# Attention of an encoder layer on one core: probabilities transposed in 64-row tiles, scores issued one at a time over three banks, chunks kept in a ring of twelve slots

## The chip, the core and the metric

The kernel runs on one core of a Trainium2 chip. The metric is the device time of one execution in microseconds (us), the median of three runs. TensorE (PE) does matmuls and transposes into PSUM, which has eight banks of 128 x 512 float32. VectorE (DVE), ScalarE (ACT) and GpSimd (POOL) work on PSUM and SBUF, SyncE issues DMAs. Each engine works through its own queue in order, and the queues are tied together by semaphores that the kernel waits on by hand.

## The reference, cut to what matters

One encoder layer over 1024 tokens of width 1024 in float32. Only the two attentions are touched by the change:

```
h = rmsnorm(x, norm1_g);  proj = h @ w_in         # queries, keys, values, pooling input
o_a = neighbourhood_attention(...)                # 4 heads of 64, 16 columns x 8 rows around each token
o_b = sliding_window_gqa(...)                     # 8 query heads on 2 key heads, |distance| <= 128, ALiBi, sink
o_c = multiscale_pool(...)
x = x + concat(o_a, o_b, o_c) @ w_out
x = x + hierarchical_moe(rmsnorm(x, norm2_g), ...)   # 32 experts, two for each token
out = rmsnorm(x, final_g)
```

For each head the attentions are softmax(q k + bias) v.

## The kernel before

The work runs in stages: projections, attention, output projection, routing, the 32 experts, the sum. Attention is a software pipeline over 96 **units**. A unit is one head of one **step**; a step is a block of 128 queries with four heads and 256 (at the edges) or 384 keys. There are 8 steps of neighbourhood attention ("na", one per block) and then 16 of sliding window attention ("swa", two groups of four heads per block). `attention_plan()` lays the work out over ticks; at tick u each engine runs its part of the list:

- PE: when u is a multiple of 4, the scores of the four units of a step (`scores`, L809 and L814): keys and queries have 64 features, heads with even number lie on partitions 0 to 63, odd ones on 64 to 127, and each unit has one of the banks 0 to 3. Unit u waits until unit u - 4 has left its bank (`bias_done`). In ticks 0, 2, 4 and 6 it still does parts of the last projection (`last_high`, L781).
- DVE: `bias_and_max(u)` (L1514, L1526) reads the scores from PSUM, adds the bias table and writes them to SBUF; the reciprocal of the sum of unit u - 2, and for some units its normalising multiply (L1550).
- ACT: the exponentials of unit u (L1177).
- POOL: the normalising multiply of the other units (L2039), three in four of swa.

Eleven to fourteen ticks after tick 4s of its scores a step comes to its transposes and its products. For each **chunk** of 128 keys PE transposes the four 128 x 128 blocks of probabilities (`transposes`, L829) into one bank (one of 4, 5, 7 in turn), DVE or ACT copies the bank to SBUF (`evacuate_chunk`, L485 and L490), and PE multiplies with the values (`times_values`, L847 for na, L853 for swa, where one product serves both groups) into bank 6; ACT copies the result out (L1190). There are 22 chunks of na and 44 of swa. The copies go to two sets of buffers, `ptna` and `ptswa`, and wait until the step two before has been multiplied (`pv_done`). In the list, the transposes of a step come first, then the products of the step before. DVE makes 25 of the 66 copies, ACT 41.

On DVE's queue the order within a tick is bias, reciprocal, multiply, and last the copy of the chunk that PE transposes in the same tick; the next tick's bias stands behind it. Two ticks after the last unit PE does the four pooling products (`pooled`, L859) into banks 0 to 3.

Of the kernel before, what the change touches and what calls it, by code (L numbers as in the profile page):

```python
# [26 lines left out]
F32 = mybir.dt.float32  # L27
# [5 lines left out]
P = 128  # L33
# [55 lines left out]
def attention_plan():  # L89


    steps = []
    for i in range(TT):
        lo, hi = max(i - 1, 0), min(i + 2, TT)
        steps.append(("na", i, 0, lo * P, (hi - lo) * P))
    for b in range(TT):
        lo, hi = max(b - 1, 0), min(b + 2, TT)
        for g in range(SWA_KV):
            steps.append(("swa", b, g, lo * P, (hi - lo) * P))
    lag = 8  # L100
    ticks = [[] for _ in range(4 * len(steps) + lag + 4)]
    late = []
    for s, (kind, i, g, k0, nk) in enumerate(steps):
        nc_ = -(-nk // P)
        items = []
        for c0 in range(0, nc_, GROUP):
            group = range(c0, min(c0 + GROUP, nc_))
            items += [("T", s, c) for c in group]
            items += late
            late = [("V", s, c) for c in group] if kind == "na" or g == 1 else []  # L110
        if s == len(steps) - 1:
            items += late
        for j, it in enumerate(items):
            ticks[4 * s + 3 + lag + (4 * j) // len(items)].append(it)
    return steps, ticks


def encoder(nc, x, norm1_g, w_in, nat_tab, swa_sink, pool_w, pool_scale, w_out, norm2_g,
# [8 lines left out]
    with ExitStack() as ctx:  # L127
# [8 lines left out]
        def sem(name):  # L136
# [62 lines left out]
        pswa = [at(f"pswa{i}", [P, 4, 3 * P + 1], F32, off) for i, off in enumerate((H + 56 * KB, TD + 8 * KB, TMP, Q + 8 * KB))]  # L199
        ptna = [at(f"ptna{i}", [P, 5, 512], F32, W + 4 * KB + i * 10 * KB) for i in range(2)]  # L200
        ptswa = [[at(f"ptswa{i}_{c}", [P, 2, 512], F32, W + 4 * KB * (1 + 3 * i + c) if 3 * i + c < 5 else Q) for c in range(3)]
                 for i in range(2)]

# [193 lines left out]

        def by_vector(n):

            return n % 2 == 0 if n < na_chunks else n % 3 == 0  # L400

        def tbank(n):

            return (4, 5, 7)[n % 3]

        VBANK = 6

        def chunk_ready(eng, n):

            if n >= 0:  # L410
                mine = by_vector(n)
                eng.wait_ge(pt_v if mine else pt_a, sum(by_vector(m) == mine for m in range(n + 1)))

# [22 lines left out]
        def sbank(u):  # L436
            return u % 4

# [36 lines left out]

        def evacuate_chunk(eng, copy, done, s, c):

            n = chunk_no[(s, c)]
            kind, i, g, k0, nk = steps[s]
            w = min(P, nk - c * P)  # L480
            eng.wait_ge(tr_done, n + 1)
            if kind == "na":
                if s >= 2:
                    eng.wait_ge(pv_done, vnum[(s - 2, last_chunk[s - 2])] + 1)
                copy(ptna[s % 2][0:w, c, :], ps[0:w, tbank(n), :]).then_inc(done, 1)  # L485
            else:

                before = NA_STEPS - 2 + i if i < 2 else NA_STEPS + 2 * (i - 2) + 1
                eng.wait_ge(pv_done, vnum[(before, last_chunk[before])] + 1)
                copy(ptswa[i % 2][c][:, g, :], ps[:, tbank(n), :]).then_inc(done, 1)  # L490

# [197 lines left out]
        def _(pe):  # L689
# [111 lines left out]
            def scores(u):  # L801
                s, h = u // 4, u % 4
                kind, i, g, k0, nk = steps[s]
                if s < NA_STEPS:
                    if u >= 4:
                        pe.wait_ge(bias_done, u - 3)
                    q = qa[(h % 2) * HD:(h % 2 + 1) * HD, h // 2, i * P:(i + 1) * P]
                    k = ka[(h % 2) * HD:(h % 2 + 1) * HD, h // 2, k0:k0 + nk]
                    mm = nc.tensor.matmul(ps[:, sbank(u), 0:nk], q, k, start=True, stop=True)  # L809
                else:  # L810
                    pe.wait_ge(bias_done, u - 3)
                    hh = 4 * g + h
                    rows = slice((hh % 2) * HD, (hh % 2 + 1) * HD)
                    mm = nc.tensor.matmul(ps[:, sbank(u), 0:nk], qs[rows, hh // 2, i * P:(i + 1) * P], kb[rows, g, k0:k0 + nk],  # L814
                                          start=True, stop=True)
                mm.then_inc(score_done, 1)

            def transposes(s, c):
                n = chunk_no[(s, c)]
                w = min(P, steps[s][4] - c * P)  # L820
                if c == 0:
                    pe.wait_ge(norm_p, sum(not norm_by_vector(u) for u in range(4 * s + 4)))
                    pe.wait_ge(norm_v, sum(norm_by_vector(u) for u in range(4 * s + 4)))
                if n == 2:
                    pe.wait_ge(proj_out, 2 * MT)
                else:
                    chunk_ready(pe, max((m for m in range(n) if tbank(m) == tbank(n)), default=-1))
                for h in range(4):
                    mm = nc.tensor.transpose(ps[0:w, tbank(n), h * P:(h + 1) * P],  # L829
                                             pbuf(4 * s + h)[:, c * P:c * P + w], ident[:])  # L830
                mm.then_inc(tr_done, 1)

            def times_values(s, c):
                kind, i, g, k0, nk = steps[s]
                oi = o_steps.index(s)
                w = min(P, nk - c * P)
                tile = k0 // P + c
                chunk_ready(pe, chunk_no[(s, c)])
                if c == 0 and oi == 0:
# [4 lines left out]
                if kind == "na":  # L844
                    for h in range(4):
                        half = slice((h % 2) * HD, (h % 2 + 1) * HD)
                        mm = nc.tensor.matmul(bank[half, (h // 2) * P:(h // 2 + 1) * P],  # L847
                                              vtok[0:w, tile, h * HD:(h + 1) * HD], ptna[s % 2][0:w, c, h * P:(h + 1) * P],
                                              start=(c == 0 and h < 2), stop=(c == last_chunk[s]), skip_group_check=True)
                else:  # L850
                    chunk_ready(pe, chunk_no[(s - 1, c)])
                    for gg in range(2):
                        mm = nc.tensor.matmul(bank[gg * HD:(gg + 1) * HD, :], vtok[:, tile, 256 + gg * HD:256 + (gg + 1) * HD],  # L853
                                              ptswa[i % 2][c][:, gg, :], start=(c == 0), stop=(c == last_chunk[s]))
                mm.then_inc(pv_done, 1)

            def pooled(i, n):
                pe.wait_ge(pool_step, POOL_OPS)
                mm = nc.tensor.matmul(ps[:, 2 * i + n, :], pwd[:, i, :], cu[:, i, PAD + n * 512:PAD + (n + 1) * 512],  # L859
                                      start=True, stop=True)  # L860
# [3 lines left out]
            pe.wait_ge(proj_out, PROJ.index((ORDER.index(3), 1)) + 1)  # L864
            pe.wait_ge(const_in, 16 * 9)
            for u, tick in enumerate(ticks):
                if u < NU and u % 4 == 0:
                    for h in range(4):
                        scores(u + h)
                if u in (0, 2, 4, 6):  # L870
# [3 lines left out]
                if u == NU + POOL_LAG:  # L874
                    pe.wait_ge(bias_done, NU)
                    for i in range(2):
                        for n in range(2):
                            pooled(i, n)
                for kind, s, c in tick:
# [235 lines left out]
        def _(act):  # L1115
# [76 lines left out]
            def wo_high(n, k):  # L1192
                c = n * KT + k
                act.wait_ge(wo_in[wo_count(c)], 32 * max(c // 4, 1))
                nc.scalar.copy(wohi[n][:, k, :], woraw[wo_buf(c)][:]).then_inc(wohi_done[n], 1)

            pending = []
            for u, tick in enumerate(ticks):
                if u < NU:
                    exponentials(u)  # L1200
                if u == NU + POOL_LAG:
                    act.wait_ge(const_in, 16 * 9)
                    for i in range(2):
                        for n in range(2):
                            act.wait_ge(pool_mm, 2 * i + n + 1)
                            nc.scalar.mul(oT[:, 6 + i, n * 512:(n + 1) * 512], ps[:, 2 * i + n, :],
                                          pscale[:, i:i + 1]).then_inc(pool_out, 1)
                for s in pending:
                    o_evacuate(s)
                pending = []  # L1210
                for kind, s, c in tick:
                    if kind == "T" and not by_vector(chunk_no[(s, c)]):
                        evacuate_chunk(act, nc.scalar.copy, pt_a, s, c)
                    if kind == "T" and chunk_no[(s, c)] == len(chunk_no) - 1:
# [164 lines left out]
        def _(dve):  # L1379
# [163 lines left out]
            for u, tick in enumerate(ticks):  # L1543
# [642 lines left out]
```

## Time and profile before

| | |
|---|---|
| median of 3 runs | 731.18 us (730.85 to 731.6) |
| the profiled execution: time, span of its instructions | 730.85 us, 729.0 us |
| mean granted TensorE clock | 0.992 |
| attention, from its first scores to its last product | 166.64 to 283.05 us of the span |
| PE busy over the span | 97% |

A granted clock of 1 means 2.4 GHz; it is 1.00 in all of attention. In the profile's rows a busy time of PE counts the matmuls' latency too, so PE can read 100% busy while it waits a little; the chain of work that ended last gives each piece only the time until the next one starts, and the pieces add up. A float32 matmul shows as two records there, a transpose as one.

### The profile page before, as it was taken

How to read it: one execution, taken by the hardware profiler on the slowest of the kernel's cores; microseconds unless marked ns; L12 is line 12 of the kernel's file. 1: busy time of each engine (PE TensorE's matmuls, PEld its weight loads, DVE VectorE, ACT ScalarE, POOL GpSimd, SP SyncE). 2: the span in 40 equal slices, each digit the busy share in tenths (PEclk: the TensorE clock that was granted, in tenths of full speed). 3: DMA queues.
4: the chain of work that ended last, by engine and by line, in shares of the span. 5: the costliest groups of instructions: out<-in, count | busy, mean ns of one | idle time of the engine just before them, and what ended most of it. 6: DMA issues, size and time to landing. Idle time of an engine off the chain costs nothing.

```text
span 729.0 us, 10252 instructions
## 1 busy us (share of the span) xinstructions
PE 704.2 (97%) x3757; PEld 511.3 (70%) x3757; DVE 508.0 (70%) x811; ACT 390.1 (54%) x585; POOL 321.8 (44%) x241
## 2 busy tenths in 40 slices
PE   7999999999999999999999899999999999999983
PEld 6888888886775556888889666666666666666631
DVE  5646422215988887214377898888888888888977
ACT  6500000104888887001122688888888888887815
POOL 2423458953778771610000454444444444442213
PEclk9999999999999999999999999999999999999997
DMA  9422112100400003705666599999999999999978
GB/s 308 140 58 58 32 55 59 30 0 23 123 1 1 1 1 140 206 5 200 230 227 207 178 351 385 390 384 381 383 383 384 390 383 383 385 386 379 400 273 350
DMA packets 62419, 157.74 MB, mean 216 GB/s; under 512 B 10168, under 2 KB 24992, under 8 KB 62368
## 3 DMA queue, kind: packets, MB, share of 16 engines
q1 hardware_dynamic: 55728, 139.58, 52.9%
q0 software_dynamic: 6336, 16.89, 7.0%
q8 instruction: 31, 0.51, 0.3%
q10 hardware_dynamic: 304, 0.59, 0.2%
q14 instruction: 20, 0.16, 0.1%
HBM read 142.36 MB, written 18.87 MB: 221 GB/s over the span
## 4 chain that ended last, share of the span: by engine, by line
PE 88%; DMA 5%; DVE 3%; SPq 1%; issue 1%; ACT 1%; POOL 0%; DVEq 0%; POOLq 0%
PE ps L1008 7%; PE ps L1013 7%; PE ps L1016 7%; PE ps L727 6%; PE ps L725 6%; PE ps L726 6%; PE ps L829 4%; PE ps L891 4%; PE ps L893 4%; PE ps L892 4%; PE ps L1039 4%; PE ps L1043 4%; PE ps L1035 4%; PE ps L814 3%; DMA wd<-in_expert_w_down 3%; PE ps L853 3%
## 5 line engine op out<-in xcount | busy, mean ns | idle before, releaser
L1810 DVE TENSOR_TENSOR wgulo<-wgu,unit 128x2048 fp32r<-128x2048 f32 x64 | 146.2, 2286 | 26.4 <-ACT unit L1276 26.4
L1276 ACT CAST unit<-wgu 128x2048 fp32r<-128x2048 f32 x64 | 122.2, 1910 | 3.7 <-PE ps L949 1.6
L2084 POOL DMA_INDIRECT expert_rows<-ysb,idx x32 | 70.8, 2212 | 108.2 <-ACT ysb L1323 107.2
L2077 POOL DMA_INDIRECT xg<-h_rows,idx x32 | 59.2, 1849 | 71.2 <-PE ps L984 58.3
L725 PE MATMUL ps<-hThi,whi 128*128 128x512 f32 x200 | 78.3, 392 | 0.0
L727 PE MATMUL ps<-hThi,wlo 128*128 128x512 f32 x200 | 77.9, 389 | 0.0
L726 PE MATMUL ps<-hTlo,whi 128*128 128x512 f32 x200 | 77.8, 389 | 0.0
L1816 DVE TENSOR_TENSOR wdlo<-wd,unit 128x2048 fp32r<-128x2048 f32 x32 | 73.1, 2285 | 2.6 <-ACT unit L1285 2.5
L1008 PE MATMUL ps<-unit,xThi 128*80 128x512 f32 x256 | 70.9, 398 | 0.8 <-ACT xThi L1300 0.8
L1013 PE MATMUL ps<-unit,xTlo 128*80 128x512 f32 x256 | 69.2, 391 | 0.0
L1016 PE MATMUL ps<-wgulo,xThi 128*80 128x512 f32 x256 | 69.1, 391 | 0.0
L1285 ACT CAST unit<-wd 128x2048 fp32r<-128x2048 f32 x32 | 61.1, 1909 | 4.8 <-DMA wd<-in_expert_w_down 4.8
L2039 POOL TENSOR_SCALAR pswa<-pswa,esum 128x384 f32<-128x384 f32 (+1 forms) x48 | 55.9, 1182 | 12.8 <-DVE esum L1533 12.8
L1137 ACT COPY kb<-ps 64x512 f32<-64x512 f32 x8 | 4.7, 583 | 92.6 <-DVE ps L1410 92.5
L1013 PEld LDWEIGHTS ps<-unit,xTlo 128*80 128x80 f32 x256 | 37.8, 148 | 21.1 <-DVE xTlo L1823 0.2
L1016 PEld LDWEIGHTS ps<-wgulo,xThi 128*80 128x80 f32 x256 | 37.8, 148 | 21.1
L891 PE MATMUL ps<-wohi,oThi 128*128 128x512 f32 x128 | 51.3, 401 | 0.0
L893 PE MATMUL ps<-wohi,oTlo 128*128 128x512 f32 x128 | 50.0, 391 | 0.0
L892 PE MATMUL ps<-wolo,oThi 128*128 128x512 f32 x128 | 49.9, 390 | 0.0
L1008 PEld LDWEIGHTS ps<-unit,xThi 128*80 128x80 f32 x256 | 35.4, 149 | 16.7 <-ACT xThi L1300 0.9
L1177 ACT ACTIVATE pswa<-pswa,mneg 128x385 f32<-128x385 f32 (+1 forms) x64 | 37.6, 588 | 13.0 <-DVE mneg L1526 12.8
L1972 POOL TENSOR_SCALAR stat<-stat 128x1 f32<-128x1 f32 x16 | 5.5, 344 | 87.8 <-ACT h L1249 65.3
(226 smaller groups left out, 1449.4 us busy)
## 6 DMA issues: line engine op xcount, KB each, us to landing
wgu<-in_expert_w_gate SPq DMA_DIRECT2D x64, 512.0 KB, 12.4
wgu<-in_expert_w_up SPq DMA_DIRECT2D x64, 512.0 KB, 15.3
wd<-in_expert_w_down SPq DMA_DIRECT2D x32, 1024.0 KB, 17.5
y<-expert_rows SPq DMA_DIRECT2D x16, 512.0 KB, 9.8
wraw<-in_w_in SPq DMA_DIRECT2D x14, 512.0 KB, 3.9
xin<-in_x SPq DMA_DIRECT2D x8, 512.0 KB, 6.7
x<-in_x SPq DMA_DIRECT2D x8, 512.0 KB, 7.3
out<-fo SPq DMA_DIRECT2D x8, 512.0 KB, 3.3
```

What stands on the lines that cost most here:

```text
L725: nc.tensor.matmul(bank, whi[i % 2][:, k, :], hThi[:, k, cols], start=(k == 0), stop=False)
L726: nc.tensor.matmul(bank, whi[i % 2][:, k, :], hTlo[:, k, cols], start=False, stop=False)
L727: mm = nc.tensor.matmul(bank, wlo[i % 2][:, k, :], hThi[:, k, cols], start=False, stop=(k == KT - 1))
L891: nc.tensor.matmul(ps[:, g % 4, :], oThi[t][:, k, :], wohi[n][:, k, :], start=(k == 0), stop=False)
L892: nc.tensor.matmul(ps[:, g % 4, :], oThi[t][:, k, :], wolo[n][:, k, :], start=False, stop=False)
L893: mm = nc.tensor.matmul(ps[:, g % 4, :], oTlo[t][:, k, :], wohi[n][:, k, :], start=False, stop=(k == KT - 1))
L1008: nc.tensor.matmul(bank, xThi[e % 2][:, 4 * a + k, :], hi[:, :, k * DE:(k + 1) * DE], start=(a == 0 and k == 0), stop=False)
L1013: nc.tensor.matmul(bank, xTlo[e % 2][:, 4 * a + k, :], hi[:, :, k * DE:(k + 1) * DE], start=False, stop=False)
L1016: mm = nc.tensor.matmul(bank, xThi[e % 2][:, 4 * a + k, :], lo[:, :, k * DE:(k + 1) * DE], start=False, stop=(a == 1 and k == 3))
L1276: nc.scalar.copy(weight_unit(e, a)[:], raw_half(wgu, e, a)).then_inc(ahi_done, 1)
L1810: nc.vector.tensor_tensor(raw_half(wgulo, e, a), raw_half(wgu, e, a), weight_unit(e, a)[:].bitcast(F32), ALU.subtract).then_inc(alo_done, 1)
L1816: nc.vector.tensor_tensor(wdlo[e % RING][:].rearrange("p j d -> p (j d)").rearrange("p (a f) -> p a f", a=2), wd[e % RING][:].rearrange("p ...
```

## The change

Four edits, all in attention:

1. Each 128 x 128 transpose becomes two, of 64 query rows each (partitions 0 to 63 and 64 to 127), written to the two banks of a pair, (3, 4) or (5, 7). Two chunks in a row share a pair: bank one then holds queries 0 to 63 of both chunks and four heads, bank two queries 64 to 127. A copy moves one such bank, after both chunks have been transposed. DVE makes 25 of these 66 copies (never the second bank of a pair), ACT 41. PE may use a pair of banks again when both copies of the pair two before are done, and the products of a chunk wait for both copies of its pair.
2. The copies go to one ring of twelve slots `pt`, one for each chunk; a slot is reused when its reader twelve chunks before is done.
3. Scores are issued one unit per tick, two ticks ahead of DVE (unit u + 2 at the head of tick u), over banks 0 to 2; a unit waits until the unit three before it has left its bank.
4. The plan puts one chunk's transposes into each of the first three ticks of a step and all products of the step before into the fourth. The fourth pooling product uses bank 0 again and comes a tick later.

```diff
-GROUP = 3
+SLOTS = 12
+AHEAD = 2
...
-        for j, it in enumerate(items):
-            ticks[4 * s + 3 + lag + (4 * j) // len(items)].append(it)
+        first = 4 * s + 3 + lag
+        for c in range(nc_):
+            ticks[first + c].append(("T", s, c))
+        ticks[first + 3] += late
+        late = [("V", s, c) for c in range(nc_)] if kind == "na" or g == 1 else []
...
-            return n % 2 == 0 if n < na_chunks else n % 3 == 0
+        def by_vector(pair, half):
+            return half == 0 and (2 * pair < na_chunks or pair % 3 != 2)
...
+        def tbanks(pair):
+            return ((3, 4), (5, 7))[pair % 2]
...
         def sbank(u):
-            return u % 4
+            return u % 3
...
+        def evacuate_pair(eng, copy, done, pair, half):
+            n = 2 * pair
+            eng.wait_ge(tr_done, n + 2)
+            if n >= SLOTS:
+                eng.wait_ge(pv_done, max(reader(n - SLOTS), reader(n + 1 - SLOTS)))
+            j = n % SLOTS
+            copy(pt[:, j:j + 2, :].rearrange("p c (h x q) -> p c h x q", h=4, x=2)[:, :, :, half],
+                 ps[:, tbanks(pair)[half], :].rearrange("p (c h q) -> p c h q", c=2, h=4)).then_inc(done, 1)
...
-                    pe.wait_ge(bias_done, u - 3)
+                    pe.wait_ge(bias_done, u - 2)
...
                 for h in range(4):
-                    mm = nc.tensor.transpose(ps[0:w, tbank(n), h * P:(h + 1) * P],
-                                             pbuf(4 * s + h)[:, c * P:c * P + w], ident[:])
+                    for half in range(2):
+                        rows = slice(half * HD, (half + 1) * HD)
+                        o = (n % 2) * 256 + h * HD
+                        mm = nc.tensor.transpose(ps[:, tbanks(pair)[half], o:o + HD],
+                                                 pbuf(4 * s + h)[rows, c * P:(c + 1) * P], ident[rows, rows])
...
+            first_units = {0: (0, 1, 2), 1: (), 2: (3, 4), 3: (), 4: (5, 6), 5: (), 6: (7, 8), 7: (9,)}
             for u, tick in enumerate(ticks):
-                if u < NU and u % 4 == 0:
-                    for h in range(4):
-                        scores(u + h)
+                for x in first_units.get(u, (u + AHEAD,)):
+                    if x < NU:
+                        scores(x)
...
-                    if kind == "T" and by_vector(chunk_no[(s, c)]):
-                        evacuate_chunk(dve, nc.vector.tensor_copy, pt_v, s, c)
+                    if kind == "T" and chunk_no[(s, c)] % 2 == 1 and by_vector(chunk_no[(s, c)] // 2, 0):
+                        evacuate_pair(dve, nc.vector.tensor_copy, pt_v, chunk_no[(s, c)] // 2, 0)
```

## Rows read from the trace of the kernel before

**Rows 1.** The page: busy time of each engine, and the granted clock in 40 slices.
```profile
PE 704.2 (97%) x3757; PEld 511.3 (70%) x3757; DVE 508.0 (70%) x811; ACT 390.1 (54%) x585; POOL 321.8 (44%) x241
...
PEclk9999999999999999999999999999999999999997
```

**Rows 2.** The chain that ended last, whole attention: start, length (us), piece.
```profile
166.71 1.06 PE ps L809 x8
...
186.39 1.02 PE ps L847 x16
...
215.58 1.02 PE ps L847 x16
...
260.07 2.73 PE ps L853 x12
```

**Rows 3.** The same chain, one block of swa (eight units).
```profile
235.08 1.49 PE ps L814 x8
236.57 2.06 PE ps L829 x16
238.63 1.98 PE ps L814 x8
240.61 0.59 PE ps L829 x4
241.20 2.72 PE ps L853 x12
243.92 0.59 PE ps L829 x4
244.51 0.52 PE ps L814
```

**Rows 4.** Busy time of each engine in that block.
```profile
235.08:244.51 9.43, 9.43 (x54) 4.98 (x54) 7.63 (x30) 7.52 (x22) 7.45 (x7) 1.00 0.01 2
```

**Rows 5.** The chain, one step of na (four units).
```profile
188.44 1.49 PE ps L809 x8
189.93 0.59 PE ps L829 x4
190.52 1.46 PE ps L847 x24
191.98 1.02 PE ps L829 x8
193.00 0.52 PE ps L809
```

**Rows 6.** The chain, end of attention.
```profile
272.81 3.44 PE ps L859 x8
...
280.47 0.59 ACT ptswa L490
```

**Rows 7.** The chain, one expert: transposes of 80 rows into 80 columns.
```profile
425.80 0.56 PE ps L984 x8
```

**Rows 8.** Timeline in the block of rows 3: start, length, engine, operation.
```profile
237.23 0.68 DVE L490 COPY ptswa<-ps 128x512 f32<-128x512 f32 x1
...
237.83 0.61 DVE L1526 CUSTOM_DVE_ANT_0 pswa<-ps,dist,nsink 128x384 f32<-128x384 f32 x1
...
238.56 0.30 PEld L814 LDWEIGHTS ps<-kb,qs 64*128 64x128 f32 x4 [0.17 <-DVE mneg L1526]
...
239.70 0.29 PEld L814 LDWEIGHTS ps<-kb,qs 64*128 64x128 f32 x2 [0.20 <-DVE mneg L1526]
...
240.54 0.42 PEld L829 LDWEIGHTS ps<-ident,pswa 128*128 128x128 f32 x4 [0.55 <-issue]
```

**Rows 9.** Timeline in na: a chunk's four transposes and DVE's copy of it.
```profile
185.74 0.66 PE L829 MATMUL ps<-ident,pna 128*128 128x128 f32 x4
...
186.43 0.69 DVE L485 COPY ptna<-ps 128x512 f32<-128x512 f32 x1
```

**Rows 10.** Groups of the attention stage by line and shape: busy us, mean ns of one.
```profile
L1526 DVE CUSTOM_DVE_ANT_0 pswa<-ps,dist,nsink 128x384 f32<-128x384 f32 x48 | 29.0, 604 | 0.4
...
L1514 DVE CUSTOM_DVE_ANT_0 pna<-ps,ti 128x384 f32<-128x384 f32 x20 | 10.9, 543 | 2.6 <-PE ps L809 2.6
```

More of the change, by code:

```diff
@@ L104, in attention_plan @@
         nc_ = -(-nk // P)
[L105 to L110, printed above, removed]
+        first = 4 * s + 3 + lag
[3 more added lines that the diff above has]
+        late = [("V", s, c) for c in range(nc_)] if kind == "na" or g == 1 else []
         if s == len(steps) - 1:
-            items += late
-        for j, it in enumerate(items):
-            ticks[4 * s + 3 + lag + (4 * j) // len(items)].append(it)
+            ticks[first + nc_ - 1] += late
     return steps, ticks
@@ L199, in encoder @@
         pswa = [at(f"pswa{i}", [P, 4, 3 * P + 1], F32, off) for i, off in enumerate((H + 56 * KB, TD + 8 * KB, TMP, Q + 8 * KB))]
[L200 to L202 removed]
+        pt = at("pt", [P, SLOTS, 512], F32, W)
         pa = at("pa", [P, S + 2 * PAD], F32, TMP)
@@ L396, in encoder, with pair_ready, reader @@
         na_chunks = sum(s < NA_STEPS for s, _ in chunk_no)
-        def by_vector(n):
-            return n % 2 == 0 if n < na_chunks else n % 3 == 0
-        def tbank(n):
-            return (4, 5, 7)[n % 3]
+        def by_vector(pair, half):
+            return half == 0 and (2 * pair < na_chunks or pair % 3 != 2)
+        def tbanks(pair):
+            return ((3, 4), (5, 7))[pair % 2]
         VBANK = 6
[L408 to L412, printed above, removed]
+        def pair_ready(eng, pair):
+            if pair >= 0:
+                n_v = sum(by_vector(m, half) for m in range(pair + 1) for half in range(2))
+                eng.wait_ge(pt_v, n_v)
+                eng.wait_ge(pt_a, 2 * (pair + 1) - n_v)
+        def reader(n):
+            s, c = next(k for k in chunk_no if chunk_no[k] == n)
+            if steps[s][0] == "swa" and steps[s][2] == 0:
+                s += 1
+            return vnum[(s, c)] + 1
         def norm_by_vector(u):
@@ L819, in transposes @@
                 n = chunk_no[(s, c)]
-                w = min(P, steps[s][4] - c * P)
+                pair = n // 2
                 if c == 0:
@@ L875, in _ @@
                     pe.wait_ge(bias_done, NU)
-                    for i in range(2):
-                        for n in range(2):
-                            pooled(i, n)
+                    pooled(0, 0)
+                    pooled(0, 1)
+                    pooled(1, 0)
+                if u == NU + POOL_LAG + 1:
+                    pooled(1, 1)
                 for kind, s, c in tick:
@@ L1202, in _ @@
                     act.wait_ge(const_in, 16 * 9)
[L1203 to L1207, printed above, removed]
+                    pooled_out(0, 0)
+                    pooled_out(0, 1)
+                    pooled_out(1, 0)
+                if u == NU + POOL_LAG + 1:
+                    pooled_out(1, 1)
                 for s in pending:
@@ L1211, in _ @@
                 for kind, s, c in tick:
-                    if kind == "T" and not by_vector(chunk_no[(s, c)]):
-                        evacuate_chunk(act, nc.scalar.copy, pt_a, s, c)
+                    if kind == "T" and chunk_no[(s, c)] % 2 == 1:
+                        for half in range(2):
+                            if not by_vector(chunk_no[(s, c)] // 2, half):
+                                evacuate_pair(act, nc.scalar.copy, pt_a, chunk_no[(s, c)] // 2, half)
                     if kind == "T" and chunk_no[(s, c)] == len(chunk_no) - 1:
```

38 lines of the change are left out of this document (15 added, 23 removed).

## The prediction

> **What bounds the kernel now.** I read the page first: PE is busy for 97% of the span at a granted clock of 1.0 everywhere but at the ends [rows 1]. That points to PE, but its busy time counts latency, so I went to the chain that ended last. Attention runs there from 166.71 to 283.05 us, nearly all of it PE [rows 2]. Then I took one steady block, eight units of swa, and looked at the pieces [rows 3]: they add up to 9.43 us, all on PE. In the same 9.43 us DVE is busy for 7.63, ACT for 7.52 and POOL for 7.45 [rows 4]. So PE sets the pace, but the three others are at 80%: a gain on PE of more than 1.8 us per block would meet them, and a small delay that falls into a loop between PE and DVE shows at once.
>
> **Prices from the rows.** Transposes: a piece of four takes 0.59 us and one of eight 1.02 [rows 5], so a chunk costs 0.43 to 0.44 (0.109 for one transpose) and 0.155 is paid once when the array goes over from another shape. Scores: in swa the last unit of a step was once held back alone; its weights came at 239.70 and the next transposes at 240.54 [rows 8]. These 0.84 us are 0.64 for the score itself, 0.10 because its weights could not be loaded beforehand, and 0.10 to empty the array. Yet four scores take 1.49 together [rows 3]: 2 x 0.64 plus 0.2 for the changes of shape. So an even and an odd head, which use different halves of the rows, run at the same time if they stand side by side in PE's queue. Products with the values: 2.72 for three chunks [rows 3], 0.85 each plus 0.17; in na 1.46 for three [rows 5], of which 0.15 is the change of shape.
>
> A block before is then: scores 2.53, 24 transposes 2.62, products 2.55, six changes of shape about 1.04, together 8.74; the other 0.69 of 9.43 are waits (0.49 in the second group of scores, 1.98 against 1.49, and 0.16 in the sixteen transposes) [rows 3].
>
> **The transposes.** Half the columns, two at a time in different halves of the rows. The trace has no such shape. Nearest is the transpose of 80 rows into 80 columns: eight in 0.56 us, 0.070 each against 0.109 for 128 columns [rows 7], so time goes with columns, and 64 columns give 0.055. If the two halves overlap as scores do, a chunk costs 4 x 0.055 = 0.22 instead of 0.44; if they do not, 8 x 0.055 = 0.44, no gain. I take 0.22, because scores of the same 64-row shape do overlap. The transposes now have the shape of the scores, so the change between them costs nothing. Per block six chunks save 1.3 us, and of 1.04 for changes of shape about 0.35 stay.
>
> The Trainium skill says the same of the shapes ("TensorEngine Tiling (Array Packing)", Tiling Modes: changing the tiling mode drains the array); the 0.155 of rows 5 agrees. It speaks for this change, and the next step is what speaks against it.
>
> **Scores one at a time.** In seven of eight places a chunk's transposes or the products stand between two scores. These transposes use both halves of the rows, and PE takes its queue in order, so the next score cannot start beside the last one. Eight lone scores are 8 x 0.632 = 5.06 us; only where a fourth tick has no products (once per block) do two stand side by side, which gives 0.63 back. Scores go from 2.53 to 4.43 per block: +1.9. PE's own work is then 4.43 + 1.14 for transposes + 2.55 for products + 0.35 = 8.5 us, against 8.74 before. All that the small transposes give is spent on lone scores.
>
> **The wait between PE and DVE.** With three banks, the score at the head of tick u + 2 waits for the bias of unit u + 1, and that stands on DVE's queue behind the copy of tick u, which waits for the transposes of tick u. From the rows: the last of four transposes starts at 185.74 + 0.055 + 3 x 0.109 = 186.12 and DVE's copy at 186.43, 0.31 later [rows 9]; from copy to next bias 0.60 (237.23 to 237.83), from there to the score's weights 0.73 (to 238.56) [rows 8]. That is 1.64 us from the last transpose to the score two ticks on. In between PE has one lone score and one chunk, 0.06 + 0.63 + 0.17 = 0.86. It stands still for 0.78, and then loads weights in the open for 0.10.
>
> A block of eight ticks in order, from the last transpose of its second tick (a copy by DVE): 0.06 third score, to 0.69; transposes to 0.86; fourth score held until 1.64, done at 2.38; array emptied, three products, emptied again, 5.17; fifth score to 5.91, transposes 6.08 (both copies here are ACT's: pair index 2 of 3); sixth score 6.71, transposes 6.94; seventh 7.57, transposes 7.74 (copy by DVE); eighth score at once, but the ninth, which should run beside it, is held until 7.74 + 1.64 = 9.38, done 10.12; transposes 10.29; tenth score 10.92, transposes 11.09. A block takes **11.1 us instead of 9.43**: PE waits 0.78 and about 1.0 in it and loses the one pair that was left. DVE, at 7.6 us of work, does not bind by its amount but by the place of its copies.
>
> In na all first banks are copied by DVE, so each step has one such hold before its products (a second one falls behind the products and is hidden). With na's bias of 0.54 instead of 0.60 [rows 10]: four lone scores 2.53, two openings 0.2, transposes 0.57, products 1.24 + 0.15, hold 0.72 + 0.10 = 5.5 us against 4.56 [rows 5]. Where scores have 256 keys both the loss from lone scores and the step are smaller, and the hold is a little longer. I take +0.9 for a step.
>
> **The other edits.** Copies keep number, size and engine (25 and 41). The write in runs of 64 elements is not in the trace; I take nothing, since writing 128 partitions x 512 with longer strides costs ACT the same in its copies to oT; its upper bound, 0.1 per DVE copy, lies in the hold and gives 2 us. The ring of twelve: a slot's reader lies about four steps back, so its wait is never last. Waiting for both copies of a pair costs nothing before products, which come one tick or more after; only the last pair, both copies by ACT, costs one more copy of 0.59 [rows 6], hidden by nothing. The last pooling product waits for a copy that is done long before: 3.44 us for the four as before [rows 6].
>
> **The sum.**
> - Start, first scores to first products (19.7 us before: 166.71 to 186.39 [rows 2]): two more groups of scores between the last projection's matmuls, 0.4 each for the changes, and five scores without a partner, 0.32 each: +2.4.
> - na, from the first products to 215.58, seven steps: 7 x 0.9 = +6.3.
> - swa, from there to the products at 260.07, five blocks: 5 x 1.67 = +8.4.
> - End: no scores left, seven chunks save 0.2 each, one more copy, some waits stay: -0.5.
>
> Together +16.6 us. The profiled execution took 730.85 us for a span of 729.0; 747.5 would be its time, and the median of the runs lies 0.3 above it: **748 us**. The stages after attention wait for it and are PE's chain too; nothing there gives time back.
>
> **Rivals.**
> - *The transposes do not overlap or run at 0.11 for a pair* (for: 16 instructions to feed in 0.22 us, which no row shows; against: rows 7). 66 chunks x 0.22 = 14 us, of which the holds cover about a third: +10, **758 us**.
> - *The halves of the array are independent*, so that a score passes by the transposes still waiting for the other half. Then lone scores cost little, but the hold of 1.64 stays in its loop: a block takes about 9.7, a na step +0.4. 5 x 0.3 + 7 x 0.4 + 1 - 0.5: +5, **736 us**. Against it: in the trace PE's matmuls start in queue order. The Trainium skill has both sides: "TensorEngine Tiling (Array Packing)", Key Properties, calls tiles independent, while "TensorE: Matmul & The Clock Gate", Part 3, says matmuls start and end in program order. The second I hold for this queue.
> - *No hold* (faster): DVE's copy never stands before a bias that PE waits for, because DVE is ahead or the sequencer's run-ahead hides it. Then a block is PE's own 8.5 (-0.9 x 5), a na step 4.68 (+0.1 x 7), start near 0 to +1, end -0.5: -3 to -4, **728 us**. It decides as soon as PE's waits in a block are below the 0.69 of today. Against it: the hold is a chain of four durations that are all in the rows, and three banks leave no more slack.
>
> **Chances.** My forecast 0.54 (its own range 742 to 754); slow transposes 0.16; independent halves, or holds half hidden, 0.19; no hold 0.11, half of it a gain that can be measured. 0.2% of the time, 1.5 us, is about what a measurement of this kernel tells from no change. Faster 0.07, same 0.05, slower 0.88. The range 736 to 759 leaves out no hold and the worst of slow transposes.
>
> **What the profile after will show.** Transposes as 64-row rows, 528 of them, a group of eight taking some 0.2 us in the chain; scores in pieces of one unit of 0.64 or 0.74 us; PE held by DVE's bias about twice a block, 1.6 us after the transposes; the chain no longer PE alone but with DVE's copy and bias in it; DVE's busy share lower; a block of swa 11.1 us and a na step near 5.5. I am wrong if two scores start together across a chunk, if the holds are missing, or if a group of eight transposes takes 0.4.

## The result, and the profile after

The changed kernel takes 751.84 us (median of four runs, 744.54 to 752.13) against 731.01 us before (median of four). The ratio is 1.0254, 95% interval 1.0222 to 1.0285: slower by 20.8 us. Run together again it gave 751.61 us against 731.60, ratio 1.0271 (1.0256 to 1.0287). The forecast was 748 us, range 736 to 759. Ratios and intervals compare fast runs alone; one run of experiment 3 and one of experiment 6 were slow, so there the ratio is not that of the medians given.

The page of the changed kernel, its busy times and its granted clock in 40 slices, to set beside [rows 1]:

```profile
PE 714.2 (95%) x4021; PEld 513.9 (68%) x4021; DVE 511.1 (68%) x811; ACT 393.1 (52%) x585; POOL 321.8 (43%) x241
...
PEclk9999999999599999999999999999999999999997
```

All engines have about the work they had; PE has 264 more matmuls (eight transposes for four) and its share is down by two points. The clock has a 5 in the slice from 188 us. That was not in the forecast. A table by stretch (length, then busy time of PE, PE's weight loads, DVE, ACT and POOL, each with the number of its instructions; granted clock; DMA share; GB/s) shows where:

```profile
174.00:182.00 8.00, 7.99 (x41) 4.89 (x41) 6.07 (x27) 4.26 (x13) 3.90 (x4) 1.00 0.12 43
182.00:186.00 4.00, 3.22 (x26) 1.48 (x23) 3.59 (x16) 3.20 (x10) 3.06 (x3) 1.00 0.95 264
186.00:190.00 4.00, 4.00 (x27) 2.39 (x25) 3.01 (x14) 2.76 (x8) 2.82 (x3) 0.54 1.00 264
190.00:203.00 13.00, 13.00 (x81) 8.03 (x81) 5.41 (x21) 5.95 (x18) 5.41 (x5) 0.50 0.05 16
```

Just before the clock fell from 2.4 to 1.2 GHz, PE was busy for 3.22 of 4 us, with lone 64-row scores and waits; in the kernel before it was busy for all 4.00 of that stretch. The clock stayed at one half from 186.3 to 203.4 us. Outside attention both kernels have a fall of 3.4 us among the experts (before: at 393 us, after: at 415), so the forecast's "1.0 everywhere but at the ends" was not quite so; it is the same on both sides.

The chain that ended last has at the places of [rows 2], first scores and the first, last-of-na and sixth group of swa products:

```profile
167.23 1.06 PE ps L807 x6
...
190.58 1.91 PE ps L848 x16
...
230.43 1.02 PE ps L848 x16
...
281.67 2.73 PE ps L854 x12
```

By stretch, in us, both profiled executions:

| stretch | before | after | difference | forecast |
|---|---|---|---|---|
| first scores to first products | 19.68 | 23.35 | +3.67 (some 4 us at half clock) | +2.4 |
| na, seven steps | 29.19 | 39.85 | +10.66 (13 us at half clock) | +6.3 |
| swa, five blocks | 44.49 | 51.24 | +6.75 | +8.4 |
| end, to the output projection (283.05, 304.14) | 22.98 | 22.47 | -0.51 | -0.5 |
| the rest of the kernel | 445.95 | 446.16 | +0.2 | 0 |

Another 0.5 us lies ahead of the first scores. One steady block of swa, which answers to [rows 3 and 4], as busy times and in the chain:

```profile
260.19:271.04 10.85, 9.54 (x79) 4.87 (x80) 8.06 (x31) 7.84 (x21) 7.39 (x6) 1.00 0.00 0
```
```profile
260.19 2.73 PE ps L854 x12
262.92 0.21 PE ps L812
...
265.62 0.69 DVE pt L487
266.31 0.07 DVE pswa L1538
266.38 0.38 issue
...
266.89 0.46 PE ps L812
...
268.85 0.69 DVE pt L487
269.54 0.52 DVE pswa L1538
...
270.13 0.91 PE ps L812 x2
```

The block takes 10.85 us instead of 9.43. The chain, all PE before, leaves PE twice: copy (265.62), bias, then a score (266.89), and again 268.85 to 270.13. In the timeline, PE's stops before these two scores name DVE's bias as what ended them:

```profile
266.89 0.59 PE L812 MATMUL ps<-kb,qs 64*128 64x384 f32 x1 [0.81 <-DVE mneg L1538]
...
270.13 0.91 PE L812 MATMUL ps<-kb,qs 64*128 64x384 f32 x2 [0.51 <-DVE mneg L1538]
```

Over all runs of the changed kernel (eight) there are two groups. Seven took 751.4 to 752.4 us with a mean clock of 0.979 to 0.983; one took 744.54 us with 0.996. Two of the seven have a profile, and both show the fall. The run without it, from here on the run at full clock, costs 13.5 us over the kernel before, the fall of the clock another 7.3. It is a single run and has no profile.

### The profile page after: what moved, and what is told of

The parts are those of the page before. It is cut to its first block, busy times and chain, and to the rows that moved or that the text cites. A ratio compares the mean times of both kernels' runs of the same rounds, so it can differ in the third digit from the quotient of the medians.

```text
span 750.3 us, 10819 instructions
## 1 busy us (share of the span) xinstructions
PE 714.2 (95%) x4021; PEld 513.9 (68%) x4021; DVE 511.1 (68%) x811; ACT 393.1 (52%) x585; POOL 321.8 (43%) x241
## 4 chain that ended last, share of the span: by engine, by line
PE 90%; DVE 3%; DMA 3%; issue 1%; ACT 1%; SPq 0%; DVEq 0%; POOL 0%; POOLq 0%; ACTq 0%
PE ps L1014 8%; PE ps L1019 8%; PE ps L1022 8%; PE ps L723 6%; PE ps L724 6%; PE ps L725 6%; PE ps L897 4%; PE ps L1045 4%; PE ps L1041 4%; PE ps L899 4%; PE ps L1049 4%; PE ps L898 4%; PE ps L830 4%; PE ps L812 3%; PE ps L854 3%; PE ps L990 2%
## 5 line engine op out<-in xcount | busy, mean ns | idle before, releaser
L812 PE MATMUL ps<-kb,qs 64*128 64x384 f32 (+1 forms) x128 | 49.0, 502 | 9.6 <-DVE mneg L1538 9.6
```

## The experiments

**1. DVE's copy behind the next tick's bias.**

```diff
+            held = []
             for u, tick in enumerate(ticks):
                 if u < NU:
                     bias_and_max(u)
+                for pair in held:
+                    evacuate_pair(dve, nc.vector.tensor_copy, pt_v, pair, 0)
+                held = []
...
-                        evacuate_pair(dve, nc.vector.tensor_copy, pt_v, chunk_no[(s, c)] // 2, 0)
+                        held.append(chunk_no[(s, c)] // 2)
```

> The changed kernel with one thing moved: DVE makes its copy of a pair of chunks one tick later, behind the bias of the next tick instead of in front of it. Theory (the hold): in the changed kernel PE stands still about 1.6 us twice in each block of eight ticks, because the score two ticks on waits for a bias that is queued behind the copy. With the copy behind the bias both holds go: a block of swa falls from 10.84 us to 9.0 or less, a na step from about 4.8 to about 4.3, and the time from 744.5 (at full clock) to 731 to 734 us. Rival (lone scores alone cost the time and the waits only fill what PE would need anyway): the block stays above 10.3 and the time above 741 us.

730.91 us (median of ten) against 731.03, ratio 0.9999 (0.9988 to 1.0011). The whole loss of the change is gone with the order of two instructions on DVE's queue. Products start at 242.62 and 251.88, so a block takes 9.26 us, the profile has no fall of the clock in attention, and the mean clock is 0.991 to 0.996 in all ten runs. The table of the same stretches:

```profile
182.00:186.00 4.00, 3.30 (x31) 1.84 (x27) 3.93 (x18) 3.57 (x12) 3.71 (x4) 1.00 0.99 280
242.62:251.88 9.26, 8.83 (x79) 4.80 (x80) 7.98 (x31) 7.52 (x22) 7.39 (x7) 1.00 0.00 0
```

The time is 13.6 us below the run at full clock, 0.1 below the 731 to 734 expected. The block fell by 1.6 us, close to the 1.8 that the forecast gave both holds, but not to the 9.0 expected: one shorter stop is left (copy at 248.05, score at 249.39).

**2. Scores two at a time.**

```diff
-                for x in first_units.get(u, (u + AHEAD,)):
+                for x in first_units.get(u, (u + 1, u + 2) if u % 2 else ()):
```

> The changed kernel with scores issued two at a time, an even and an odd head side by side, at every odd tick, instead of one per tick; banks and copies as changed. Theory (lone scores plus the hold): two heads run together again, four pairs of 0.64 us instead of eight scores, and only one of the two holds per block is left (the one before the first pair of a block), so a block of swa takes 8.6 to 9.3 us and the time is 731 to 736 us. Rival (the halves of the array overlap anyway, so lone scores cost nothing): the block stays at 10 or more, the time at 741 or more.

735.11 us, ratio 1.0062 (1.0043 to 1.008): within the expectation. The block between products at 234.05 and 243.78 takes 9.73 us, a little more than expected. One hold is left in its chain (copy at 239.92, score at 241.20). So the edit takes away the lone scores and one of the two holds together, and is no test of the lone scores by themselves. It takes back more than half of the loss, experiment 1 all of it.

**3. The transposes undone alone.**

```diff
-            copy(pt[:, j:j + 2, :].rearrange("p c (h x q) -> p c h x q", h=4, x=2)[:, :, :, half],
-                 ps[:, tbanks(pair)[half], :].rearrange("p (c h q) -> p c h q", c=2, h=4)).then_inc(done, 1)
+            copy(pt[:, j + half, :], ps[:, tbanks(pair)[half], :]).then_inc(done, 1)
...
-                    for half in range(2):
-                        rows = slice(half * HD, (half + 1) * HD)
-                        o = (n % 2) * 256 + h * HD
-                        mm = nc.tensor.transpose(ps[:, tbanks(pair)[half], o:o + HD],
-                                                 pbuf(4 * s + h)[rows, c * P:(c + 1) * P], ident[rows, rows])
+                    mm = nc.tensor.transpose(ps[:, tbanks(pair)[n % 2], h * P:(h + 1) * P],
+                                             pbuf(4 * s + h)[:, c * P:(c + 1) * P], ident[:])
```

> The changed kernel with the transposes undone alone: 128 x 128 transposes, one chunk into each bank of a pair; ring, plan, waits and scores one at a time as changed. Theory: a chunk costs PE 0.44 instead of 0.22 us and the array changes shape before and after each chunk (0.155 and 0.2), which is +0.5 us for each of six chunks in a block, part of it inside the holds; a block takes 12.5 to 13.5 us, the time is 758 to 766 us. Rival (the small transposes gain nothing): within 3 us of the changed kernel at the same clock.

782.85 us (771.95 to 787.90, ratio 1.0637, interval 1.0555 to 1.0719), where the range went to 766; the single run at full clock took 771.95, 27 us more than the changed kernel at full clock. The chain in one block:

```profile
283.98 0.84 PE ps L811 x2
284.82 0.59 PE ps L826 x4
285.40 0.84 PE ps L811 x2
286.24 0.58 PE ps L826 x4
```

A lone score and a chunk take 0.84 + 0.59 = 1.43 us, where the small transposes have 0.76 to 0.87. The block of 13.51 us was expected at 12.5 to 13.5. The small transposes, with the changes of shape that they save, are a gain of 2.7 us per block here, not a cost.

**4. Both 1 and 2.**

> Both of the edits before together: scores in pairs at odd ticks and DVE's copy behind the next bias. Theory: PE's own work in a block is 4 x 0.65 for scores, 1.3 for transposes, 2.55 for products and about 0.35 for changes of shape, 6.8 us, so DVE (7.63 busy), ACT (7.52) and POOL (7.45) bind: a block takes 7.8 to 8.4 us instead of 9.43 in the kernel before, and the time is 720 to 726 us, faster than the kernel before. Rival (another wait takes the place, as the twelve slots or two pairs of banks): the block stays at 8.9 or more and the time at 729 or more.

730.73 us, ratio 0.9998 (0.9988 to 1.0009). The rival was right: the block takes 9.54 us, no less than with one of the edits. The timeline of that block, DVE:

```profile
243.04 0.15 DVE L1545 RECIPROCAL esum<-esum 128x1 f32<-128x1 f32 x1
...
244.83 0.35 DVE L1535 COPY pswa<-nsink 128x4 f32<-128x4 f32 x1 [1.63 <-PE ps L812]
...
245.22 0.62 DVE L1538 CUSTOM_DVE_ANT_0 pswa<-ps,dist,nsink 128x384 f32<-128x384 f32 x1
```

During the products (241.23 to 243.95) DVE runs out of scores, which stand behind them in PE's queue. It is idle for 1.63 us, until the first score after them is done; in the next part of the block PE waits for DVE. The waits from 240 to 262 us, in all, times, longest:

```profile
PEld ps L812 <- DVE mneg L1538: 5.0, 9, 0.8
```

That these waits set the block is argued from the two views; the next experiment, which was to remove them, did not confirm it.

**5. Pairs at even ticks, just ahead of the products.** As 4, but:

```diff
-            first_units = {0: (0, 1, 2), 1: (), 2: (3, 4), 3: (), 4: (5, 6), 5: (), 6: (7, 8), 7: (9,)}
+            first_units = {0: (0, 1, 2), 1: (), 2: (3, 4), 3: (), 4: (5, 6), 5: (), 6: (7, 8), 7: (9,), 8: (10, 11)}
...
-                for x in first_units.get(u, (u + 1, u + 2) if u % 2 else ()):
+                for x in first_units.get(u, () if u % 2 else (u + 2, u + 3)):
```

> Scores in pairs as before and DVE's copy behind the next bias, but the pairs at even ticks (units u + 2 and u + 3, which wait for the bias of the same tick u), so that a pair stands right ahead of the products and DVE has three units to work on during their 2.7 us. With pairs at odd ticks DVE stood idle for 1.6 us during the products and PE then waited for it, and a block took 9.54 us. Theory (DVE starved during the products sets that block): the block falls to 8.4 to 9.0 us, the time to 723 to 728 us. Rival (what is gained is lost again before the pair, which now waits for the bias of its own tick): block 9.4 or more, time 730 or more.

748.85 us, ratio 1.0258 (1.0202 to 1.0314). The rival came, and by more than it said: the block takes 10.64 us (products at 244.27 and 254.91). In its chain the copy stands before a bias that a score waits for once more:

```profile
252.03 0.69 DVE pt L487
...
253.34 0.60 DVE pswa L1538
...
254.00 0.91 PE ps L812 x2
```

From copy to score are 1.97 us, and the products come behind. A pair that waits for the bias of its own tick puts a hold back, late copy or not.

**6. The scores' edit alone, on the kernel before.** The fourth pooling product comes a tick later, as in the change; all else as before.

```diff
-            return u % 4
+            return u % 3
...
-                    pe.wait_ge(bias_done, u - 3)
+                    pe.wait_ge(bias_done, u - 2)
...
-                if u < NU and u % 4 == 0:
-                    for h in range(4):
-                        scores(u + h)
+                for x in first_units.get(u, (u + 2,)):
+                    if x < NU:
+                        scores(x)
```

> The kernel before with the edit of the scores alone: one unit per tick, two ahead, over banks 0 to 2; transposes 128 x 128, copies, plan and buffers as before. Theory: scores cost 5.06 instead of 2.53 us in a block, each stands between transposes of another array shape (0.35 for going and coming back, some six times a block instead of three), and the waits for the bias behind DVE's copies come on top: a block of swa takes 12 to 13 us, the time is 752 to 768 us. Rival (the loss of the change came from the pairs of banks and the plan, not from the scores): under 740 us.

774.19 us (768.36 to 781.38, ratio 1.0554, interval 1.0484 to 1.0624); its two runs at a clock of 0.993 and 0.994 took 770.05 and 768.36, a little over the range of 752 to 768. The profile is of the longest run, with the clock at one half for 34.1 us from 237; the blocks behind that stretch, at full clock, take 12.85 us, as expected. In their chain the same pieces of 0.84 and 0.59 follow each other as in 3. So the scores' edit alone costs 37 to 38 us at full clock, and the rest of the change gives 23 to 25 of them back; by experiment 3 that is the small transposes above all.

**7. The late copy on the kernel before.** The edit of 1:

```diff
-                        evacuate_chunk(dve, nc.vector.tensor_copy, pt_v, s, c)
+                        held.append((s, c))
```

> The kernel before with DVE's copy of a chunk put behind the next tick's bias, nothing else. Theory: in the kernel before PE waits 0.65 us in a block of 9.43, 0.49 of them for DVE's bias; moving the copy back frees at most half of it, 0.2 to 0.4 us per block: 728.5 to 730.5 us. Rival (four banks of scores give enough slack, or the later copy now holds up the transposes that need its bank): 731 or more.

733.29 us, ratio 1.0023 (1.0009 to 1.0037): the rival came. With four banks of scores and single banks for the transposes the late copy is a small loss, 1.6 us, where it gave 13.6 in experiment 1.

**8. Matmuls added where the clock fell.**

```diff
+                if u in (12, 13, 14, 16, 17, 18):
+                    pe.wait_ge(proj_out, 2 * MT - 1)
+                    for _ in range(2):
+                        nc.tensor.matmul(ps[:, VBANK, 384:512], ident[:], ident[:], start=True, stop=True)
```

> The changed kernel with twelve matmuls added that nothing reads: two of identity by identity (128 x 128, some 0.22 us each) before the scores of ticks 12, 13, 14, 16, 17 and 18, around the place where the granted clock fell to one half at 186.3 us in three runs of four. They need the array's full shape, 0.35 us of changes of shape for each of the six places, so they cost 2 to 5 us where PE has no wait to hide them. Theory (the clock falls because PE does little there: lone 64-row scores with waits between them): no fall in this stretch in any run, all runs within 745 to 750 us. Rival (the clock's fall has nothing to do with what PE does there): the fall still comes in most runs and these take 753 us or more.

749.58 us (747.71 to 751.56), ratio 1.0241 (1.0206 to 1.0276). All four runs have a clock of 0.992 to 0.995, and the profiled one has no fall in attention; two of them lie up to 1.6 us above the range, so the added work cost 3 to 7 us against 744.54, where 2 to 5 were expected. The same stretch as above:

```profile
182.00:186.00 4.00, 4.00 (x30) 2.58 (x27) 2.58 (x12) 2.52 (x8) 2.91 (x3) 1.00 0.96 284
256.96:267.81 10.85, 9.54 (x79) 4.87 (x80) 8.07 (x31) 7.85 (x21) 7.40 (x6) 1.00 0.01 2
```

With PE busy in all of it, the clock stayed up. The block of swa is 10.85 us, as in the changed kernel, so the filling changed nothing there.

**9. and 10. The scores of the kernel before with the small transposes over three banks**, without and with the late copy.

```diff
-            return ((3, 4), (5, 7))[pair % 2]
+            return tuple((4, 5, 7)[(2 * pair + half) % 3] for half in range(2))
...
-            return u % 3
+            return u % 4
...
-                elif n % 2 == 0:
-                    pair_ready(pe, pair - 2)
+                if n % 2 == 0 and pair >= 1:
+                    copies = [(m, x) for m in range(pair) for x in range(2)][:2 * pair - 1]
...
-                for x in first_units.get(u, (u + AHEAD,)):
-                    if x < NU:
-                        scores(x)
+                if u < NU and u % 4 == 0:
+                    for h in range(4):
+                        scores(u + h)
```

> The 64-row transposes, the ring and the plan of the change, but the scores as in the kernel before (four units of a step side by side over banks 0 to 3), and the transposes over the three banks 4, 5, 7: the half-banks of the pairs take them in turn, and a pair of chunks waits for the copy three half-banks back. Theory: the small transposes give their 1.3 us and the shape changes 0.7 us per block, and neither lone scores nor the three-bank hold are there; PE's own work is about 6.8 us per block and DVE, ACT and POOL with 7.5 to 7.7 set the pace, so a block takes 8.2 to 9.0 us and the time is 721 to 728 us. Rival (PE's waits grow to what the transposes gave, since a pair waits for a copy only three half-banks back): a block of 9.3 or more, 730 us or more.

> The same with DVE's copy behind the next tick's bias. In the kernel before this cost 1.6 us, because the later copy held up the transposes that needed its bank. Theory: three banks for the transposes again, so it costs again: 1 to 4 us slower than the same without it. Rival (the bias in front matters more): 1 to 3 us faster.

740.24 us (1.0105, 1.0086 to 1.0124) and 750.21 us (1.0261, 1.023 to 1.0293). Both theories' times missed: 9 is 12 us above its range, where its rival put it, and the late copy costs 10 us, not 1 to 4. In the chain of 9, block 249.53 to 259.54:

```profile
248.32 0.70 DVE pt L487
249.02 0.04 issue
249.07 0.46 PE ps L834 x8
249.53 2.73 PE ps L858 x12
252.26 0.39 PE ps L834 x8
252.65 0.75 PE ps L812 x4
253.40 0.16 DVE pswa L1539
```

PE's busy time in this block is 7.52 us, so its work did shrink as planned, but a chunk's transposes wait for DVE's copy, the scores wait behind them, and DVE waits for the scores. The waits from 215 to 275 us:

```profile
DVE pswa L1539 <- PE ps L812: 11.8, 9, 4.0
PE ps L834 <- DVE pt L487: 11.6, 10, 1.7
```

The block takes 10.01 us. The clock falls here too: in attention from 183.1 us for 10.2 us and from 234.3 for 6.8 in 9, and in four places for 17.1 us together in 10.

**11. The changed kernel again.**

> The changed kernel unaltered, for the granted clock. Theory: the runs fall into two groups, 744 to 745 us with a mean clock of 0.996 or near it, and 751 to 753 us with 0.98, and nothing between, since the clock stays at one half for 17 us or does not fall at all in attention. Rival (the spread has another cause): times spread between the groups, or a clock that does not go with the time.

Four runs of 751.37 to 752.37 us with 0.981 to 0.983; its profile shows the fall at 185.5 us for 17.1 us. No run of the eight lies between the groups, as the theory said, but only one of them is in the shorter one.

**12. All copies by ACT.**

```diff
-            return half == 0 and (2 * pair < na_chunks or pair % 3 != 2)
+            return False
...
-                eng.wait_ge(pt_v, n_v)
```

> The changed kernel with all 66 copies of the transposed chunks on ACT, none on DVE; all else as changed. Theory (the hold is made by the copy's place on DVE's queue): with no copy there, the holds go as they do when it is moved behind the bias; PE's own 8.9 to 9.1 us set a block, ACT has 7.5 + 2 x 0.47 = 8.5 and stays under it, DVE falls to 6.4; a block takes 9.0 to 9.4 us and the time is 728 to 732 us, with no fall of the clock in attention. Rival (ACT becomes the bound, since its copies and the exponentials queue behind each other): a block of 9.8 or more, 735 us or more.

730.71 us (eleven runs, 729.67 to 731.89) against 731.64, ratio 0.9991 (0.9981 to 1.0). Two blocks, between products at 241.19, 250.56 and 259.71, take 9.37 and 9.15 us. Time, block and the missing fall are as expected. Taking the copy off DVE's queue frees what moving it behind the bias freed. ACT is busy for 9.01 of 10 us there:

```profile
240.00:250.00 10.00, 9.66 (x79) 5.36 (x78) 7.72 (x32) 9.01 (x28) 8.02 (x8) 1.00 0.00 0
```

The lowest of all, 12, is 0.1% below the kernel before, and its interval reaches 1.0: no version beats that kernel by more than the measurement can tell.

## Why the prediction was right

**The hold was right, and it decides.** The forecast put two holds into a block, each about 1.64 us from the last transposes to the score two ticks on: 0.31 from the transposes to the copy and 1.33 from there to the score [rows 8 and 9]. The trace has copy to score in 266.89 - 265.62 = 1.27 and 270.13 - 268.85 = 1.28, and 0.27 from the last transpose to the copy each time, 1.54 in all. Experiment 1 leaves DVE's work as it is and changes only the place of the copy, experiment 12 takes the copy away from DVE; both bring the block to 9.26 on average. PE's stops before the two scores are shorter than forecast, 0.81 and 0.51 where the forecast had about 1.0 and 0.78.

**Lone scores were right.** They cost what was worked out: 0.84 with the change of shape in experiments 3 and 6, the same number as in [rows 8]. The forecast also said that they would eat what the small transposes give, so that PE's own work would stay about the same (8.5 against 8.74 before). Experiment 1 bears this out: lone scores kept, holds gone, and the block takes 9.26 against 9.43. Experiment 2 gets back 9.4 us against the run at full clock, but with the lone scores it takes away a hold. Both mechanisms close one loop: a score, its bias, the copy, the next score. Shortening either part frees the loop until another wait binds, and 1 and 2 together give no more than 1 alone. This the forecast had not worked out; it named the loop but priced its parts as a sum. Which wait sets the block then (experiment 4) stays open.

**The transposes were right in size, and wrong in their place.** In one half of the array they follow each other 0.062 us apart, against 0.055 in the forecast: in the row of five below, 0.47 us in all, less 0.22 for the last one's own time, is four steps. What the forecast had wrong is how they stand to the scores. The first score after the products starts at 262.85, the next at 263.61 (a float32 score shows as two records):

```profile
262.85 0.59 PE L812 MATMUL ps<-kb,qs 64*128 64x384 f32 x1
262.86 0.40 PE L830 MATMUL ps<-ident,pswa 64*128 64x64 f32 x3
263.28 0.48 PE L812 MATMUL ps<-kb,qs 64*128 64x384 f32 x1
263.28 0.27 PE L830 MATMUL ps<-ident,pswa 64*128 64x64 f32 x1
...
263.60 0.22 PE L830 MATMUL ps<-ident,pswa 64*128 64x64 f32 x1
263.61 0.59 PE L812 MATMUL ps<-kb,qs 64*128 64x384 f32 x1
263.66 0.47 PE L830 MATMUL ps<-ident,pswa 64*128 64x64 f32 x5
...
264.36 0.28 PE L830 MATMUL ps<-ident,pswa 64*128 64x64 f32 x3
```

The rows do not name the half, but the queue does: the eight transposes of a chunk take the two halves in turn. Four run beside the first score, the other four start when it is through, beside the next score. Had each waited for the one ahead of it in the queue, at most one could have run beside the first score. The trace also marks the transpose that signals the end of its chunk, the last of the eight in the queue. In 21 of the 66 chunks it starts before three others of its chunk; in the second chunk of this stretch it is one of the three at 264.36, and others start up to 264.54. A score passes too: the one of 263.61 starts before the last transpose of the chunk ahead of it, 263.78. So the step "PE takes its queue in order" failed, and with it, for the starts of PE's matmuls, the sentence above that each engine works through its queue in order. The signals do keep the order: that of the second chunk comes at 264.78, when the last of the eight that started is through, and not when its own transpose is (264.63).

Two scores of different halves did not start together, which the rival of independent halves would have allowed: they start 0.71 to 0.87 us apart where no hold stands between them, although at 263.61 DVE had already done the bias that the score needs. Why transposes pass and the next score does not stays open. That rival was half right, for the small pieces only. For the starts the Trainium skill, "TensorE: Matmul & The Clock Gate", Part 3 (matmuls start and end in program order), differs from this trace, and the trace decides; for the ends the signals agree with it.

**The terms of the sum.** A block takes +1.42 instead of +1.67 (five: 6.75 against 8.4). The term that was mis-sized is a score together with its chunk where no hold stands between two scores: 0.80 to 0.91 in the forecast, 0.71 to 0.87 in the trace. There are five of these in a block, 4.34 against 3.97. The two holds and the stretch with the products come to 6.75 in the forecast and 6.89 in the trace. A na step at full clock, from 206.28 to 230.43 for five steps against 20.50 before, takes +0.73 instead of +0.9. The end is -0.51, as forecast. The run at full clock is 13.5 us longer where the sum had 16.6; with seven na steps of +0.73 that leaves some 1.5 for the start, for which no profile at full clock without added work exists, against 2.4.

**The clock was not in the forecast.** 7.3 us of the measured 20.8 come from it. The 748 us lie between the two groups of runs, 744.5 and 751.8: the sum was 3.5 us too long for the run at full clock, and a fall that it did not have put 7.3 on top. That the median came out within 4 us is in part luck. Experiment 8 shows that the fall depends on what PE does there: by the mean clock none of its four runs has a fall in attention, where seven of eight of the changed kernel do. Lone scores alone do not bring it on, since experiments 1 and 12 keep them and their profiles show no fall in attention, nor are they needed, since 9 has none of them and two falls. In the profiles of 3, 6, 9 and 10 the clock is at one half for 17 to 34 us of attention, in that of 5 for twice 3.4 us; in 4 there is no fall and in 2 one of 3.4 us, at 251 us. What the condition is, and why the fall is missing in one run of eight, stays open.

**The other rivals.** No hold is refuted by the chain. Slow transposes are refuted by experiment 3, where the full ones cost more, and by three chunks in a row at the end of attention, 0.073 us for a pair of transposes:

```profile
292.46 0.88 PE ps L830 x24
```

The longer strides of the copies, at which the forecast put nothing, cost nothing that shows: 0.69 us for DVE's, where the kernel before has 0.68 and 0.69 [rows 8 and 9]. Four banks for scores together with two pairs for the transposes and one for the products would be nine, one more than PSUM has.

## What to carry to other kernels

Where one engine feeds another through a few banks, follow the loop and not the busy shares: here swapping two instructions on DVE's queue, which changes no engine's work, was worth 13.6 us at full clock. Taking a bank from one product to buy pairs for another shortens the lead of the first, and then the order of the next queue counts: with four banks of scores the same swap cost 1.6 us. And an engine that becomes lighter does not get faster if it then waits: in experiment 9 PE is busy for 75% of a block, the block is longer than in the kernel before, where it is busy for all of it, and the clock falls as well.

## What the runs showed of the hardware that was not expected

- A fall of the granted clock to one half that lasts 17.1 us and begins behind a stretch in which PE is still busy for 80% of the time (3.22 of 4 us). Both profiles of the changed kernel have it, at 186.3 and 185.5 us; the mean clock of seven of eight runs fits it, and it is worth 7.3 us. With 4.00 of 4 us in that stretch (experiment 8) it did not come in four runs. With 3.30 of 4 us (experiment 1) it did not come in ten runs either, so the busy share alone does not tell it.
- 64 x 64 transposes of one half of the rows start before others, ahead of them in the queue, that wait for a score in the other half: in 21 of 66 chunks the last one in the queue starts before three others. The next score starts before the last transposes ahead of it (263.61 against 263.78), but not together with the score before it (0.71 to 0.87 us apart). The signal at the end of a chunk still comes only when all eight are through (264.78).
- Lone scores between full transposes pay for the change of shape each time, in experiments 3 and 6 as in the kernel before: 0.84 us for a score and 0.59 for a chunk, against 0.71 to 0.87 for the two together where the shapes agree.
